# Down product of chunks 0 and 1: Strassen's seven products instead of plain steps

## What is computed

```python
z = rmsnorm(x, norm_g) @ w_in            # three groups of heads: gMLP, attention, mLSTM
x = x + concat(A, B, C) @ w_out
h = rmsnorm(x, g) @ w_up                 # 2 * D_FF columns
h = causal depthwise conv of width 3 (h)
x = x + (gelu(h[..., :D_FF]) * h[..., D_FF:]) @ w_down
```

## Time and profile before

| | us |
|---|---|
| median of 3 runs | 2414.6 |
| lowest, highest | 2407.47, 2414.71 |
| span of the profiled execution | 2412.5 |
| busy: PE, PEld | 2388.8, 2354.2 |
| busy: DVE, ACT, POOL | 1537.0, 1089.3, 525.9 |
| mean granted TensorE clock | 0.998 |

### The profile page before, as it was taken

How to read it: one execution, slowest core, us unless ns; L and a number is a source line. 1 busy time by engine, 2 the same in 40 slices (tenths; PEclk the granted TensorE clock), 3 DMA queues, 4 the chain that set the end, 5 groups by cost and what they waited for, 6 DMA issues and landing times.

```text
span 2412.5 us, 42567 instructions
## 1 busy us (share of the span) xinstructions
PE 2388.8 (99%) x16827; PEld 2354.2 (98%) x16827; DVE 1537.0 (64%) x2697; ACT 1089.3 (45%) x2095; POOL 525.9 (22%) x578
## 2 busy tenths in 40 slices
PE   9999999999999999999999999999999999999999
PEld 8999998999999999999999999999999999999999
DVE  3115687888788876465611256877887888764454
ACT  6325676544333433343423366655333333333453
POOL 0001254432222220010110013452322222200110
PEclk9999999999999999999999999999999999999999
DMA  4442432212222223554524334321222222255564
GB/s 157 133 142 91 147 111 53 72 64 81 72 81 64 81 72 129 189 174 160 194 73 140 119 125 136 100 63 51 81 81 72 75 69 79 74 173 178 169 195 145
DMA packets 245177, 269.15 MB, mean 112 GB/s; under 512 B 16470, under 2 KB 215028, under 8 KB 242804
## 3 DMA queue, kind: packets, MB, share of 16 engines
q1 hardware_dynamic: 244980, 266.43, 34.8%
HBM read 216.27 MB, written 50.11 MB: 110 GB/s over the span
## 4 chain that ended last, share of the span: by engine, by line
PE 91%; issue 3%; DVE 3%; ACT 2%; POOL 1%; DMA 0%; POOLq 0%; DVEq 0%; ACTq 0%
PE bank L327 28%; PE bank L329 28%; PE bank L328 28%; PE bank L1167 1%; PE bank L1092 1%; PE bank L1137 1%; PE bank L1177 1%; PE bank L1124 0%; PE bank L1154 0%; DMA rawB<-in_w_down 0%; PE bank L1027 0%; PE bank L1032 0%; ACT wzH L1489 0%; POOL wN L1950 0%; PE bank L1184 0%
## 5 line engine op out<-in xcount | busy, mean ns | idle before, releaser
L327 PE MATMUL bank<-actH,wb 128*128 128x384 f32 (+1 forms) x1712 | 560.2, 327 | 1.4 <-DVE actL L2334 1.2
L328 PE MATMUL bank<-actL,wb 128*128 128x384 f32 (+1 forms) x1712 | 554.8, 324 | 0.0
L329 PE MATMUL bank<-actH,wb 128*128 128x384 f32 (+1 forms) x1712 | 554.6, 324 | 0.0
L327 PE MATMUL bank<-wzH,actH 128*128 128x256 f32 (+3 forms) x1296 | 369.5, 285 | 2.8 <-issue 1.5
L329 PE MATMUL bank<-wzH,actL 128*128 128x256 f32 (+3 forms) x1296 | 364.2, 281 | 0.0
L328 PE MATMUL bank<-wzL,actH 128*128 128x256 f32 (+3 forms) x1296 | 363.9, 281 | 0.0
L327 PEld LDWEIGHTS bank<-actH,wb 128*128 128x128 f32 x1712 | 322.4, 188 | 6.1 <-issue 3.2
L328 PEld LDWEIGHTS bank<-actL,wb 128*128 128x128 f32 x1712 | 323.2, 189 | 0.7
L329 PEld LDWEIGHTS bank<-actH,wb 128*128 128x128 f32 x1712 | 323.1, 189 | 0.0
L327 PEld LDWEIGHTS bank<-wzH,actH 128*128 128x128 f32 (+1 forms) x1296 | 236.3, 182 | 4.9 <-issue 2.1
L327 PE MATMUL bank<-tH,wb 128*128 128x384 f32 x704 | 237.0, 337 | 1.2 <-ACT vn L1864 1.2
(11 more groups left out here) (320 smaller groups left out, 5034.0 us busy)
## 6 DMA issues: line engine op xcount, KB each, us to landing
raw<-in_w_up SPq DMA_DIRECT2D x88, 512.0 KB, 4.4
raw<-in_w_down SPq DMA_DIRECT2D x88, 512.0 KB, 3.6
g_scratch<-cv SPq DMA_DIRECT2D x44, 545.0 KB, 3.1
rawz<-in_w_in SPq DMA_DIRECT2D x22, 1024.0 KB, 5.4
zb<-z_scratch SPq DMA_DIRECT2D x16, 1156.0 KB, 5.9
tHf<-g_scratch SPq DMA_DIRECT2D x88, 192.0 KB, 3.6
z_scratch<-zst SPq DMA_DIRECT2D x128, 128.0 KB, 1.8
raw<-in_w_out SPq DMA_DIRECT2D x128, 128.0 KB, 2.9
```

The source lines that it names most:

```text
L327: pe.matmul(out, aH, bH, start=first, stop=False)
L328: pe.matmul(out, aH, bL, start=False, stop=False)
L329: return pe.matmul(out, aL, bH, start=False, stop=last)
```

## The change

Chunks 0 and 1 of the down product become one product of 2 x 2 blocks and seven products in place of eight. The output rows are cut in halves (m: columns 0 to 511 and 512 to 1023 of `w_down`), the inner dimension in even and odd tiles f = 2j + k, the positions in chunks 0 and 1. One product runs over j = 0 to 10; one `unit(p, h, j)` is one j of it: 4 x 3 = 12 matmuls of 384 columns into banks 4h to 4h + 3. Products go in passes: p = 0, 1, 2 run two products (h = 0 and 1) with their units taking turns, p = 3 runs the seventh alone.

```diff
+                def unit_sums(p, h, j):
...
+                    if (u, 0) in POOL_SUM:
+                        if p < 2:
+                            pool.wait_ge(ld_in[t % 3], ld_at(l, t))
+                        x, y, op = W_SUMS[p, h]
+                        pool.tensor_tensor(w_slot(p, h, j, True)[:, 1], w_block(j, *x), w_block(j, *y), op).then_inc(s_r, 1)
+                    if (u, 1) in POOL_SUM:
+                        pool.wait_ge(ld_in[t % 3], ld_at(l, t))
...
+                        pool.tensor_tensor(g_slot(p, h, j, True)[:, 1], raw_g[:, x], raw_g[:, y], op).then_inc(s_r, 1)
...
+                def unit_low_parts(p, h, j):
...
+                    if u in DVE_SUM:
+                        dve.wait_ge(mm, slot_free(l, p, h, j))
+                        dve.wait_ge(ld_in[t % 3], ld_at(l, t))
...
+                        dve.tensor_tensor(g_slot(p, h, j, True)[:, 1], raw_g[:, x], raw_g[:, y], op).then_inc(s_l, 1)
+                    count = unit_low(l, p, h, j)
+                    dve.wait_ge(w_h, count - 1)
...
+                    dve.tensor_tensor(a[:, 1], src, a[:, 0].bitcast(F32), ALU.subtract).then_inc(w_l, 1)
+                    dve.wait_ge(w_h, count)
...
+                    dve.tensor_tensor(g[:, 1], src, g[:, 0].bitcast(F32), ALU.subtract).then_inc(w_l, 1)
+
+                def add_product(p, h, ms=range(4)):
+
+                    for m in ms:
+                        dve.wait_ge(mm, unit_mm(l, p, h, NJ - 1, m))
+                        for a, c, op in TARGETS[p, h]:
+                            x = xT[:, 4 * a + m, CH[c][0]:CH[c][0] + 384]
+                            dve.wait_ge(bank_free, F0 + 3 * KT + BEFORE[p, h, m, a, c])
+                            dve.tensor_tensor(x, x, bank[4 * h + m][:, 0:384], op).then_inc(bank_free, 1)
...
+        def slot_free(l, p, h, j):
+
+            t = NJ * p + j
+            if t < 3:
+                return tile_mm(l, NF - 1, (2, 6, 9)[t])
+            if p < 3:
+                return unit_mm(l, (t - 3) // NJ, h, (t - 3) % NJ)
+            if j < 3:
+                return unit_mm(l, 2, *((1, NJ - 2), (1, NJ - 1), (0, NJ - 2))[j])
+            return unit_mm(l, 3, 1, j - 3)
...
-                for i in range(4, 3 * NF):
+                for i in range(NF):
                     down_low(i)
                     gate_low(i)
```

More of the change, by code:

```diff
@@ new lines, in build @@
+        TARGETS = {(0, 0): ((1, 0, ALU.add), (1, 1, ALU.subtract)), (0, 1): ((0, 0, ALU.add), (1, 0, ALU.add)),
+                   (1, 0): ((0, 1, ALU.add), (0, 0, ALU.subtract)), (1, 1): ((0, 0, ALU.add),),
+                   (2, 1): ((1, 1, ALU.add),), (2, 0): ((0, 0, ALU.add), (1, 1, ALU.add)), (3, 1): ((0, 1, ALU.add), (1, 1, ALU.add))}
+        ADD_NO, BEFORE, X_ADDED = {}, {}, {}
+        count = 0
+        for (p, h), blocks in TARGETS.items():
+            for m in range(4):
+                for a, c, _ in blocks:
+                    count += 1
+                    BEFORE[p, h, m, a, c] = X_ADDED.get((c, 4 * a + m), 0)
+                    X_ADDED[c, 4 * a + m] = count
+                ADD_NO[p, h, m] = count
@@ new lines, in _ @@
+                for p, h, j in UNITS:
+                    unit(p, h, j)
+                    if (p, h, j) == (0, 0, 0):
+                        pe.wait_ge(cvs_r, (l + 1) * 4 * NF)
+                        for s in range(2):
+                            q = pe.transpose(bank[7][0:88, s * P:(s + 1) * P],
+                                             convst[:, 2 * s:2 * s + 2].rearrange("p r a -> p (r a)"), ident[:, :])
+                        q.then_inc(stt_r, 1)
+                    if (p, h, j) == (3, 1, NJ - 2):
+                        pe.wait_ge(bank_free, product_out(l, 2, 0, 3))
+                        norm_sum(pe, 2 * l + 2, 0)
@@ new lines, in step @@
+                def step(f):
+                    t0, w = CH[2]
+                    h, lo = (t.rearrange("p k n -> p (k n)") for t in down_place(f)[0:2])
+                    pe.wait_ge(w_l, down_at(l, f))
+                    pe.wait_ge(b_l, gate_at(l, f))
+                    for m in range(KT):
+                        if f == 0:
+                            pe.wait_ge(bank_free, product_out(l, *((3, 1) if m >= 4 else (2, 0)), m % 4))
+                            if m == 3:
+                                pe.wait_ge(ms_r, ms_at(2 * l + 2, 0))
@@ L1864, in _ @@
                 act.activation(cvo, bank[7][0:88, 0:256].rearrange("p (s t) -> p s t", s=2), ACT.Copy).then_inc(sto_r, 1)
+                n = 2 * l + 2
+                for p, h, j in UNITS[4:]:
+                    unit_high(p, h, j)
+                    if (p, h) == (1, 0) and 4 <= j < 8:
+                        norm_square(act, n, 0, j, x_added(l, 0, j), j - 4)
+                    if p == 3 and 3 <= j < 7:
+                        norm_square(act, n, 0, j - 3, x_added(l, 0, j - 3), j + 1)
                 def half_high(j):
@@ L2508, in _ @@
                         weights_low(p + 1, 0)
-                    elif not ahead:
-                        down_low(0)
                     dve.wait_ge(copy_r, copy_at(l, 7 + p))
@@ L2541, in _ @@
                         sum_low(p + 1, 3)
+                    else:
+                        unit_low_parts(0, 1, 0)
                 value_end(NF - 1)
-                down_low(3)
+                for p, h, j in UNITS[4:]:
+                    unit_low_parts(p, h, j)
+                    if j == 1 and 1 <= p < 3:
+                        add_product(p - 1, h)
+                    if (p, j) == (3, 0):
+                        add_product(2, 1)
+                    if (p, j) == (3, 2):
+                        add_product(2, 0)
                 n = 2 * l + 2
```

548 lines of the change are left out of this document (345 added, 203 removed).

## The result

The changed kernel takes **2464.79 us** (median of four runs, 2462.21 to 2466.37) against 2413.49 of the kernel before beside it: a ratio of 1.0217 [1.0201, 1.0233]. It is slower, as forecast, but by 51 us where the prediction had 27.

The account below looks back on a forecast made before the run. TensorE's matmuls bound the old kernel; VectorE's and GpSimd's serial work would bound passes 1 and 2. Losses of 36.5 us less 23.05 saved gave +13.4 a layer, +27 in two: 2441 us, likeliest range 2425 to 2465.

Parts of the forecast that it names:

- entry, start and pass 0: Down product's beginning: first units ready at 949.9 against 949.8 wanted, pairs then keep pace; 1.5 us lost a layer.
- pass 1, with the turn before it: Second pass of the down product: 16 adds and pairs of 4.85 us against 4.19 of TensorE; 12.7 us lost.
- pass 2: Third pass of the down product: 12 adds and pairs of 5.7 us against 4.19 of TensorE; 17.3 us lost.
- pass 3: Seventh product alone: 12 adds and units of 1.95 us, 26.9 us against 23.05 of TensorE; 3.8 us lost.
- third chunk: Down product's third chunk: first step waits for banks behind the 8 last adds; 1.2 us lost.
- matmuls saved: Chunks 0 and 1 of the down product: 132 fewer matmuls a layer at 0.1746 us, 23.05 us saved.
- rival (b): Down product: saved matmuls decide, exclusion costs nothing in passes 1 and 2; 2371 us, chance 0.08.
- Exclusion between VectorE and GpSimd: Down product: VectorE operations with two SBUF inputs and GpSimd's exclude each other, durations add; pass 2 pair 5.7 us.
- rival (d): Pass 2: TensorE's waits also lower its clock, a pair taking about 8.4 us; 2465 to 2500 us, chance 0.11.
- Rival (c): Down product: all low ends hold, gain and loss cancel, every add hidden, no gap; 2409 us, chance 0.15.
- The other signs: Down product: TensorE waits some 70 us for low parts, GpSimd's 512-wide sums take 1.7 to 2.0 us, low parts double.
- rival (a): The forecast itself: both engines' serial work sets passes 1 and 2; 2425 to 2465 us, chance 0.66.

Follow-up runs that it names:

- the last kernel: Changed kernel with sums on VectorE, except the first four units and passes 1 and 2's first two chunk pairs; adds one unit earlier: 2407.54 us, 0.9973 of the kernel before.

## Why the prediction was right in sign and short in size

Term by term, for the first layer. Stall is time above 46.1 us a pass (23.05 in pass 3), from the first matmul of each pass.

| term | predicted (low to high) | measured |
|---|---|---|
| entry, start and pass 0 | 1.5 (0.5 to 4) | 1.7 + 6.9 = 8.6 |
| pass 1, with the turn before it | 12.7 (7.4 to 18.9) | 20.7 |
| pass 2 | 17.3 (14.5 to 25.1) | 16.7 |
| pass 3 | 3.8 (0.7 to 7.8) | 4.9 |
| third chunk | 1.2 (0 to 2.5) | -1.3 |
| sum | 36.5 | 49.6 |
| less the matmuls saved | -23.05 | -23.05 |
| a layer | +13.4 | +26.5 |

The trace agrees with the last line: the first matmul behind the down product stands at 1233.20 instead of 1206.83, 26.4 us later; by the end of the second layer it is 50.1.

- **Matmuls saved: right.** 264 fewer, and 2370.7 us when GpSimd's sums are out of the way, the very 2371 of rival (b). One small thing was missed: a pair that doesn't wait takes 4.24 us, not 4.19, some 1.6 us in the three passes of a layer, and that is in the table's stalls.
- **Exclusion between VectorE and GpSimd: right.** It was read off two waits, gave 5.7 us for a pair of pass 2 and was measured at 5.61 in the three steady pairs, where whole durations would have added to 6.23. The kernel before with idle sums shows the longer low parts without a chain. That the whole of pass 2 came out as forecast (17.3 and 16.7) is in part luck: the other eight pairs were shorter and longer, and in the second layer, with four pairs at 4.24, it was 14.7. The Trainium skill (SBUF — State Buffer, section "SBUF: two separate sides") calls the pair of ports an exclusive lock; the trace agrees, and adds from PSUM stayed outside it, as the earlier trace rows had said: eight of them from 998.82 took 3.79 us, as they do alone, though two GpSimd sums (998.44 to 1001.26) lay beside the first five.
- **Start: the step that failed first.** I asked when unit (0,0,2) would be ready *behind* the gate product and took that product's end, 948.8, from a trace in which GpSimd was idle there. The exclusion was applied to the new instructions only. But it holds VectorE's old ones too: taps and product of 1.35, 1.35 and 1.30 us took 2.00, 1.99 and 2.26, and counted from the entry the product ended 3.3 us later. The row of entry, start and pass 0 is 7.1 us of the 13.1 that a layer came out worse. Of its 8.6 us, 3.3 are the wait behind the product, 1.9 two waits for low parts sBr at 964.24 and 967.58, and 1.7 the later entry, which isn't shown to be the change's. With the sums of the later units on VectorE the taps and the product took 1.35, 1.35 and 1.29 again and the wait was 1.6 us instead of 3.3.
- **Pass 1: the step that failed second.** The sum there was the busy time of both engines less 5 us of adds hidden beside sums. It held only the serial work. Three things were missing: the wait of 3.8 to 4.0 us at the turn (I had foreseen "3 us or more in one piece", but gave it no term of its own), the idle time of VectorE behind the chain of sum, copy and low part, and the clock. The chain is seen in two rows of pass 1:

```profile
1036.47 6.08 POOL L2300 TENSOR_TENSOR sAf<-wrA 128x512 f32<-128x512 f32 x4
1038.83 1.04 DVE L2730 TENSOR_TENSOR sA<-sAf,sA 128x512 fp32r<-128x512 f32 x1 [1.90 <-ACT sA L1983]
```

  GpSimd makes four sums in a row while VectorE idles for the first of them; over the kernel VectorE waited 47.2 us for copies of summed weights. Of the eleven pairs of pass 1 three took 4.24, 4.29 and 4.80 us and the others 5.1 to 7.5, 5.71 in the mean, so my 4.85 was the length of one. How the excess divides among the shared turn, the chain and the clock no run shows.
- **Clock: rival (d) was right in kind and small in size.** It came down where TensorE had waited 2.5 to 4 us in one piece: 0.75 and 0.57 after 996.00, 0.69 after a wait of 2.5 at 1038.95, 0.74 after one of 3.0 at 1059.78. In 1001 to 1006 nineteen matmuls filled 5.00 us without a gap, where 19 x 0.1746 = 3.3 would do, so 1.7 us are lost there; a mean of 0.93 over pass 1 is at most 4.4 us. It was 0.70 after two waits of 0.8 and 2.0 us close together, from 1112.49. But it stayed at 1.00 over the wait of 3.28 at 952.43, and in the steady pairs of pass 2, where one gap of 1.0 us and smaller ones made 1.4 us of idle time in each 5.6. The same wait at the start was followed by the low level in three other executions. Stretch 955 to 960 of the changed kernel, and of the run with one sum moved, whose wait was 3.5 us:

```profile
955.00:960.00 5.00, 4.29 (x24) 4.29 (x25) 3.87 (x8) 0.19 (x1) 0.00 (x0) 1.00 0.97 270
955.00:960.00 5.00, 5.00 (x21) 5.00 (x21) 2.33 (x5) 0.00 (x0) 0.49 (x1) 0.68 0.96 306
```

  With the adds early it was 0.66 after a wait of 3.3, and with narrow adds 0.55 after one of 3.4. So whether a wait of this length costs the clock differs between executions. The Trainium skill (TensorE: Matmul & The Clock Gate, section "What's actually happening") ties the half clock to an array that idled; the trace agrees in that each fall in the down product stood behind such waits, though not each such wait was followed by a fall. The prediction had named a clock row under 1.00 in pass 2 as a sign of being wrong, and it was 0.95: what it had in mind, the short pauses of the steady pairs, cost no clock, but the longer waits at the pass's start and near its end did. A term for it was missing; the run without GpSimd's sums has the clock at 1.00 all through, but no run here changed the clock alone, so its share stays a bound.
- **Rival (c)**, 2409, needed every add hidden and no gap at a turn. Leaving the adds out brought 12.8 of the 56 us above it, so the greater part was the waits at the start, the turns and behind the chain.
- **Pass 3 and the third chunk** were within their bounds, or 1.3 us under.
- **The other signs.** PE's waits for low parts and adds were 62.5 us (some 70 forecast), but 19.0 of them were for the adds; the wait of over 3 us at the start of pass 1 came. GpSimd's 512-wide sums took 1.54 us in the mean, under the 1.7 to 2.0 forecast, and of the 308 low parts 112 took more than 1.0 us, not all of them double. Pairs of pass 0 that didn't wait took 4.24.

So the sign and the mechanism were right, and the time lies in the stated range, but near its end: 2464.79 is at the upper end of rival (a), and the loss is nearly twice the one forecast.

My expectations missed in three ways that are worth telling. For the kernel with all sums on VectorE I had the string right (4.3 us a pair in pass 2, measured 4.28) and took only 5 to 10 us of waiting a layer, where a string level with TensorE leaves adds with no cover: the kernel lost 21.5 us a layer against the one without GpSimd's sums. For one sum moved I expected a gain by operation, where the ring of three made each round wait for the same GpSimd sum. And for the early adds I gave 5 to 8 us a layer if their queue was the cause of the wait; it moved to the next low parts, as the other branch of that expectation had it.

Between its two down products the changed kernel was 1.6 us quicker than the one before, in work that the change doesn't touch (1233.20 to 2153.00 against 1206.83 to 2128.23). No run here explains it; single executions of the kernel before differ by up to 7 us. The second layer's part is then 25.3 us, close to the first's 26.4.

## What to carry to other kernels

Before work goes to an idle GpSimd, look for places in the old trace where a VectorE and a GpSimd instruction with SBUF operands overlap: if the one is longer than alone, their times add, and busy shares (64% and 22% here) say nothing about room. Apply that to VectorE's old instructions in the stretch as well as to the new ones, look at what is queued on GpSimd behind the new work and who waits for it, and compare the whole string, its own work and what it lets through, with the bound engine's step. If it comes level, everything that stands in it only now and then, such as adds at a change of products, lies bare. VectorE's adds from PSUM ran at full pace beside GpSimd's sums here, so sums on GpSimd cost least beside them; that the 0.3% of the last kernel came of this isn't shown.

## What the runs showed of the hardware

- VectorE operations with two SBUF inputs and GpSimd's sums alternate one for one when both have work: in the kernel before with extra sums each low part (0.55 or 1.22 us alone) took 1.1 us longer, whatever number of sums was queued, and GpSimd's sums went from 1.30 to a median of 1.49 and a mean of 1.70. The 1.1 us is the same for both lengths, so many short operations lose more than few long ones.
- Adds of VectorE with a PSUM operand don't take part, 0.474 us each with or without a GpSimd sum beside them. That was expected from the earlier trace rows. Two thirds of the adds' 37.7 us cost the changed kernel nothing; the prediction had some 14 of 19 us of them hidden in passes 1 to 3.
- TensorE's granted clock was 0.57 in the mean of 5 us after a wait of 4.0 us, and 0.69 and 0.74 in stretches around the ends of waits of 2.5 and 3.0. After a wait of 3.3 to 3.5 us at one and the same place it was 1.00 in one execution and 0.68, 0.66 and 0.55 in three others. It stayed at 1.00 where TensorE idled 1.4 us in every 5.6, one gap of 1.0 us among it.
- Loads at 242 GB/s and 73% of the DMA engines' time, over a whole pass, didn't make TensorE wait when GpSimd's sums were gone.
